# Late tokens of the output and down projections: the high and the low part of the activations in one product of 512 columns

## What is computed

```python
mix = jnp.concatenate([attn, pooled.astype(attn.dtype)], axis=-1) @ p['w_out']
x = x + gt1 * mix
h2 = rms_norm(x, p['norm2_g']) * (1.0 + sc2) + sh2
x = x + gt2 * conv_ffn(h2, p['w_up'], p['conv_w'], p['conv_b'], p['w_down'])
```

## Time and profile before

| | |
|---|---|
| time, median of 3 runs | 1441.02 us (1440.68 to 1443.09) |
| span of the profiled execution | 1439.4 us |
| lowest time of a run less this span | 1.3 us |
| TensorE (PE) busy | 1407.3 us, 98% |
| VectorE (DVE) busy | 903.1 us, 63% |
| ScalarE (ACT) busy | 534.1 us, 37% |
| GpSimd (POOL) busy | 400.5 us, 28% |
| DMA | 147.05 MB, mean 102 GB/s |

### The profile page before, as it was taken

One profiled execution on the slowest core, in us unless ns is written; L12 is line 12 of the kernel. 1 busy time (PEld: TensorE's weight loads), 2 busy tenths in 40 slices (PEclk: granted clock), 3 DMA queues, 4 the chain that ended last, 5 costly groups with the idle time before them and its releaser, 6 DMA issues.

```text
span 1439.4 us, 25053 instructions
## 1 busy us (share of the span) xinstructions
PE 1407.3 (98%) x9905; PEld 1353.2 (94%) x9905; DVE 903.1 (63%) x1429; ACT 534.1 (37%) x798; POOL 400.5 (28%) x273
## 2 busy tenths in 40 slices
PE   6999999999999999999999999999999999999997
PEld 4888889999999999999999977999999999999997
DVE  4448869897966478785775787369744323444333
ACT  5436862533231123232242587344233112232322
POOL 0264002153440033433205800214433101323321
PEclk9999999999999999999999999999999999999999
DMA  9752005253535334335423200224323312222321
GB/s 315 248 178 80 1 2 161 81 166 106 164 121 162 94 117 145 120 120 153 120 58 86 63 1 2 59 89 132 104 79 90 87 57 67 73 73 73 101 61 74
DMA packets 198158, 147.05 MB, mean 102 GB/s; under 512 B 4400, under 2 KB 187448, under 8 KB 197048
## 3 DMA queue, kind: packets, MB, share of 16 engines
q1 hardware_dynamic: 196592, 144.27, 32.8%
q10 hardware_dynamic: 1480, 1.57, 0.3%
HBM read 142.94 MB, written 2.88 MB: 101 GB/s over the span
## 4 chain that ended last, share of the span: by engine, by line
PE 87%; DVE 7%; ACT 2%; issue 2%; SPq 1%; DMA 1%; DVEq 0%; ACTq 0%
PE pair L1468 68%; PE pair L1484 7%; PE pair L1865 3%; PE pair L1910 3%; PE pair L1879 2%; DVE mod_acc L1050 1%; DVE in_lo L1116 1%; DVE norm_t L1106 1%; SPq L414 1%; DVE conv L1390 1%; DMA w_first<-in_w_mod_dram 1%; DVE w_lo L1027 1%; DVE small L1328 1%; PE pair L1768 1%; PE pair L1720 1%
## 5 line engine op out<-in xcount | busy, mean ns | idle before, releaser
L1468 PE MATMUL pair<-in_hi,w_hi 128*128 128x384 f32 x1728 | 396.1, 310 | 0.2
L1468 PE MATMUL pair<-in_lo,w_hi 128*128 128x384 f32 x1728 | 394.7, 309 | 0.0
L1468 PE MATMUL pair<-in_hi,w_lo 128*128 128x384 f32 x1728 | 392.7, 308 | 0.0
L1390 DVE SCALAR_TENSOR_TENSOR conv<-pair,vec,conv 128x127 f32<-128x127 f32 x352 | 168.7, 541 | 193.4 <-ACT conv L935 192.9
L1468 PEld LDWEIGHTS pair<-in_hi,w_hi 128*128 128x128 f32 x1728 | 265.4, 189 | 5.6 <-issue 2.2
L1468 PEld LDWEIGHTS pair<-in_lo,w_hi 128*128 128x128 f32 x1728 | 265.6, 189 | 0.0
L1468 PEld LDWEIGHTS pair<-in_hi,w_lo 128*128 128x128 f32 x1728 | 263.6, 188 | 0.0
L636 POOL TENSOR_TENSOR silu_a<-silu_a,conv 128x640 f32<-128x640 f32 x44 | 113.0, 2567 | 534.2 <-DVE conv L1390 534.2
L935 ACT ACTIVATE conv<-pair,vec 128x640 f32<-128x640 f32 x88 | 77.8, 886 | 407.5 <-PE pair L1468 405.3
L1027 DVE TENSOR_TENSOR w_lo<-w_raw,w_hi 128x1024 fp32r<-128x1024 f32 (+1 forms) x148 | 195.7, 1322 | 38.4 <-ACT w_hi L658 37.9
L658 ACT ACTIVATE w_hi<-w_raw 128x1024 fp32r<-128x1024 f32 (+1 forms) x82 | 96.9, 1182 | 287.1 <-PE pair L1468 270.5
(11 more groups left out here) (205 smaller groups left out, 1775.5 us busy)
## 6 DMA issues: line engine op xcount, KB each, us to landing
w_raw<-in_w_up_dram SPq DMA_DIRECT2D x88, 512.0 KB, 3.8
mod_raw<-in_w_mod_dram SPq DMA_DIRECT2D x64, 512.0 KB, 4.4
w_raw<-in_w_down_dram SPq DMA_DIRECT2D x32, 704.0 KB, 4.6
w_raw<-in_w_in_dram SPq DMA_DIRECT2D x20, 512.0 KB, 4.2
w_first<-in_w_mod_dram SPq DMA_DIRECT2D x16, 512.0 KB, 8.8
w_raw<-in_w_out_dram SPq DMA_DIRECT2D x16, 512.0 KB, 4.1
mod_raw<-in_w_mod_dram SPq DMA_DIRECT2D x4, 1024.0 KB, 5.1
mod_acc<-in_w_mod_dram SPq DMA_DIRECT2D x4, 1024.0 KB, 5.0
```

Of the source, the lines that this page charges most:

```text
L1390: ins = dve.scalar_tensor_tensor(out=conv[:, s, d0:d1], in0=up_result(g, j, s)[:, d0 + sh:d1 + sh], scalar=v(L, V_TAP[t], s * NF + g * FG ...
L1468: ins = pe.matmul(dst[:, a:e], w[:, s, k, :], rhs[:, kk, a:e], start=first and r == 0, stop=last and r == 2)
```

## The change

In the output and down projections, and there only in the tiles that `linear` made (tiles 0 to 5 where a norm follows, 0 to 7 otherwise), the two passes with w_hi over tokens 384 to 639 become one matmul. Its moving operand is the high and the low part of these 256 tokens side by side (for which the two SBUF tensors become one, `in_parts` and `act_parts`), 512 columns, and its result is a whole PSUM bank: columns 0 to 255 of it take w_hi * high (and later w_lo * high), columns 256 to 511 take w_hi * low alone. Five matmuls for one block k, 1,920 columns as before. The low product of the late tokens is thus no longer summed in PSUM with the rest: VectorE adds it to x by an instruction of its own, 256 columns wide, ahead of the two that were there, and the second of these waits for it. `last_two`, `first_three`, the input and up projections and the attention stay.

```diff
+    LATE = T - EDGE
...
-            in_hi = sb("in_hi", [P, NK, T], F32R, at=inputs)
-            in_lo = sb("in_lo", [P, NK, T], F32R, at=inputs)
+            in_parts = sb("in_parts", [P, 2, NK, T], F32R, at=inputs)
+            in_hi, in_lo = in_parts[:, 0, :, :], in_parts[:, 1, :, :]
...
-                act_hi = sb("act_hi", [P, FG, T], F32R, at=own)
-                act_lo = sb("act_lo", [P, FG, T], F32R, at=own)
+                act_parts = sb("act_parts", [P, 2, FG, T], F32R, at=own)
+                act_hi, act_lo = act_parts[:, 0, :, :], act_parts[:, 1, :, :]
...
+        both = [pair[i][:, LIN0 + EDGE:LIN0 + EDGE + 2 * LATE].rearrange("p (r t) -> p r t", r=2) for i in range(2)]
+        late_low = [pair[i][:, LIN0 + T:LIN0 + T + LATE] for i in range(2)]
...
-            def residual(N, s, L, ch, m):
+            def residual(N, s, L, ch, m, g=None):
 
                 dve.wait_ge(s_lin, N + 1)
+                at = n_xlow(L, g, m)
+                dve.scalar_tensor_tensor(out=x[:, m, EDGE:T], in0=late_low[s], scalar=mod[:, L, ch, 1, m:m + 1],
+                                         in1=x[:, m, EDGE:T], op0=ALU.mult, op1=ALU.add).then_inc(s_xlow, 1)
                 for ci, a, b in SEG:
+                    if ci == 1:
+                        dve.wait_ge(s_xlow, at + 1)
                     ins = dve.scalar_tensor_tensor(out=x[:, m, a:b], in0=lin[s][:, a:b],
...
+            def linear_two(n, s, nk, parts, wait_k=None, order=None):
+
+
+                pe.wait_ge(s_wlo, n + 1)
+                order = list(order or range(nk))
+                for k in order:
+                    if wait_k is not None:
+                        wait_k(k)
+                    first, last = k == order[0], k == order[-1]
+                    for r in range(2):
+                        pe.matmul(lin[s][:, 0:EDGE], w_hi[:, s, k, :], parts[:, r, k, 0:EDGE], start=first and r == 0,
+                                  stop=False)
+                    pe.matmul(both[s], w_hi[:, s, k, :], parts[:, :, k, EDGE:T], start=first, stop=False)
+                    for a, e in HALVES:
+                        ins = pe.matmul(lin[s][:, a:e], w_lo[:, s, k, :], parts[:, 0, k, a:e], start=False, stop=last)
+                ins.then_inc(s_lin, 1)
...
-                    linear(tile_out(L) + m, m % 2, NK, in_hi, in_lo, wait_k=out_wait if m == 0 else None,
-                           order=range(NQ) if m == 1 else out_order)
+                    linear_two(tile_out(L) + m, m % 2, NK, in_parts, wait_k=out_wait if m == 0 else None,
+                               order=range(NQ) if m == 1 else out_order)
...
-                        linear(down + m, m % 2, FG, act_hi, act_lo,
-                               wait_k=(lambda k: pe.wait_ge(s_alo, done + k + 1)) if m == 0 else None)
+                        linear_two(down + m, m % 2, FG, act_parts,
+                                   wait_k=(lambda k: pe.wait_ge(s_alo, done + k + 1)) if m == 0 else None)
```

More of the change, by code:

```diff
@@ L228, in build @@
                 conv = sb("conv", [P, 2, T], at=own)
-                act_hi = sb("act_hi", [P, FG, T], F32R, at=own)
-                act_lo = sb("act_lo", [P, FG, T], F32R, at=own)
+                act_parts = sb("act_parts", [P, 2, FG, T], F32R, at=own)
+                act_hi, act_lo = act_parts[:, 0, :, :], act_parts[:, 1, :, :]
                 silu_a = sb("silu_a", [P, T], at=own)
-                w_own_up = [act_lo[:, :, :].rearrange("p g t -> p (g t)")[:, T + i * NK * P:T + (i + 1) * NK * P]
+                w_own_up = [act_lo.rearrange("p g t -> p (g t)")[:, T + i * NK * P:T + (i + 1) * NK * P]
                             .rearrange("p (k n) -> p k n", k=NK) for i in range(6)]
@@ L268, in build @@
         s_lin, s_free = sem("lin_done"), sem("lin_free")
+        s_xlow = sem("x_late_low_added")
         s_gain, s_mfirst = sem("gain_ready"), sem("first_used")
@@ L364, in up_result, with n_xlow @@
             return lin[2 + s if g == 0 and isinstance(j, int) and j == 1 else s]
+        def n_xlow(L, g, m):
+            return L * (3 * NK - 4) + (m if g is None else NK - 2 + g * NK + m)
         def e_of(n):
@@ L945, in up_iter @@
                         act_e.activation(silu_a[:, :], conv[:, 0, :], ACT.Silu).then_inc(s_silu, 1)
-                    up_iter(0, tile_up(L, g) + 2, NK)
-                    up_iter(1, tile_up(L, g) + 4, NK)
+                    for j in range(2):
+                        up_iter(j, tile_up(L, g) + 2 * j + 2, NK)
                     with act_e.Fori(2, FG - 1) as j:
@@ L1416, in _ @@
                     for m in range(NK - 2 if g == NG - 1 else NK):
-                        residual(down + m, m % 2, L, 5, m)
+                        residual(down + m, m % 2, L, 5, m, g)
                         if down + m + 2 < DEPTH * PER_LAYER:
```

## The result

The changed kernel takes 1443.77 us (median of 20 runs, 1442.12 to 1445.26), the kernel before 1441.75 us in the same comparisons (20 runs, 1440.49 to 1443.77). The ratio is 1.0014, with a 95% interval of 1.0007 to 1.0020: slower by 0.14%, some 2.0 us, and less than the 0.2% that the prediction took for the bound. It had said 1439.7 us, 1.3 us faster: the sign is wrong. That 1443.8 still lies inside its range, which ends at 1444.0, is no merit of its sum: the range had been stretched towards the third rival.

What follows compares the result with a forecast made beforehand. PE was taken to bound the kernel, with VectorE setting the pace in layer 0's output projection. PE's -3.5 and VectorE's +2.2 gave -1.3 us, so 1441.0 becomes 1439.7 us; range 1436.8 to 1444.0.

Steps and rivals of the forecast that it cites:

- third rival: Down-tile blocks: wide streams dearer per column, 512 at 233.3 ns, 384 at 176.7; +3.4 us, 1444.4 us; chance 0.11.
- the price of the wide matmul: Edited PE blocks: a matmul of 512 columns was put at 213.3 + 13.3 = 226.7 ns.
- The flat 13.3: PE matmul streams: each matmul costs 13.3 ns beyond its columns at 2.4 GHz, whatever its width.
- The saving on PE: Output and down projections: one matmul of six fewer per block, 10 ns saved in each of 352 blocks, 3.5 us.
- first rival: Edited blocks: the price is mostly gone in the wide product; at 20 ns saved, -4.8 us, 1436.2 us; chance 0.13.
- second rival: Edited blocks: nothing to speak of saved, -2 to 5 ns; +0.4 to +2.9 us, 1442.3 us at 2.5 ns; chance 0.14.
- VectorE in layer 0: Output projection of layer 0: the extra additions lie on the path, +2.2 us, period 8.55 us in place of 8.14.
- The covers: Down projections and layer 1's output projection: extra additions of 0.41 us hidden by ScalarE's wait, VectorE's idle time and slack.
- The two runs of 256 columns: Wide matmul's operand: its two halves lying apart in SBUF cost nothing, read from a near case of 592 ns both ways.
- The clock: Output projection of layer 0: more PE idle time could lower the granted clock; +1.8 us, 1442.8 us and up; chance 0.03.
- Span and time: Whole kernel: the median of the runs was taken as 1.6 us above the span, 1438.1 us becoming 1439.7 us.

Runs made afterwards that it cites:

- experiment 3: Changed kernel with down tiles from the second on replaced by streams of matmuls of one width or other orders, results left out; 1445.5 us, one time.
- experiment 7: Changed kernel plus a GpSimd wait in layer 1, another order of the five matmuls, and layer 0's output projection undone; 1439.44 us against 1441.26, ratio 0.9989.
- experiment 2: Changed kernel with layer 0's output projection back to six matmuls and two additions; 1440.38 us against 1440.76, ratio 0.9999.
- experiment 9: Changed kernel once more, no edit, for a second trace; 1441.52 us beside 1442.13 for the kernel before, one run each.
- experiment 8: Changed kernel with down tiles replaced by streams of more fp32r widths and of bfloat16, results left out; 1446.35 us, one time.
- experiment 5: Changed kernel with one more GpSimd wait, letting VectorE's low weights go first in layer 1; 1441.96 us against 1441.26, ratio 1.0005.

## Why the prediction was wrong

- **The step that failed is the price of the wide matmul:** "The flat 13.3 fits three of four streams, so I take 213.3 + 13.3 = 226.7 for 512 columns." It takes 233.4 (experiment 3). The 384 of the same stream had been at 176.7 in the earlier trace rows, and I charged that to one of three. Of the three streams that "fit", 256 columns alone say nothing about wider ones. The mix in `linear` gives 13.3 by a share of its mean width, 320, just as well, and its 384 was put at 173.4 by subtraction: by the starts in the trace of the kernel before, the matmuls of 384 columns in a down tile take some 176 ns on the average and those of 256 some 117.5. Only `first_three` has 384 columns at 173.3, and no run explains why it is 3.4 ns cheaper there than in `last_two` and in experiment 3. In the changed kernel the wide matmul takes 230 to 233 ns, and the rest of the block 643 to 647 where the prediction had 643.3. Of the 10 ns that a slow block lies above the forecast 870, some 6.5 are the wide matmul; the 3.3 ns of a fast block, 873.3, are the wide matmul alone.
- **The saving on PE,** forecast at 10 ns a block and 3.5 us: measured 0 or 6.7 ns a block, by the stream. That was 0.55 us in the first trace of the change, some 1.8 in the second, and 2.05 at most (experiment 7).
- **The third rival** had the right mechanism, "wide streams are dearer per column", its prices of 233.3 and 176.7 within 0.1 ns, and a total of 1444.4 close to the 1443.8 measured. It did not have the right sum: a block of five costs 880 or 873 and not 883.4. In the slow block the 384 and 256 with w_lo take 293 ns together in place of 296.7; in the fast one the two 384s and the wide one are shorter too, 349 and 230 ns. Its total was near by luck: it had +3.4 us over the kernel before where +2.0 was measured, 1.0 of that from a term that it didn't have, and the kernel before stood 0.7 us higher in this comparison than in the three runs that it started from.
- **The first rival,** 20 ns saved a block because the wide matmul hides its price, is out: beyond its columns at 2.4 GHz a matmul of 512 costs 20.1 ns, and one of 256 to 384 costs 13.3 to 16.7.
- **The second rival,** that little is saved, gives 1442.3 with +1.3. Its sum was nearer than the forecast's, since little was saved indeed. The rule of the Trainium skill that stood beside it is right in that the fixed cost is well under 13.3 ns. No run here shows 2.5 ns: a straight line through the streams of 256 and 512 columns leaves 6.6 ns for a matmul of no columns, and the rate of 0.4583 leaves none. The same page ("TensorE: Matmul & The Clock Gate", section "Back-to-back issue gap") gives about 131 ns for a matmul of 512 columns in a sustained stream with weight loads. The trace disagrees: 233.4 ns.
- **VectorE in layer 0:** +2.2 forecast, +2.18 measured, period 8.55 forecast and 8.55 seen; undoing it alone takes it away (experiment 2). Right in size, place and mechanism.
- **The covers:** the down tiles show no wait for the residual or low weights, ScalarE's wait shrank to nothing and PE has no gap; the output projection of layer 1 hides its additions too. Right.
- **The two runs of 256 columns** cost nothing. Right, 233.4 both ways.
- **The clock** stayed at 1.00 in the output projection of layer 0, where PE has 4 us idle now. Right to leave it out.
- **What no step had:** 1.0 us in layer 1, in a stage that the change doesn't touch, half of what was measured in the end. Together: -3.5 forecast on PE became -0.55 to -1.8, +2.2 stayed, +1.0 came in, so +1.4 to +2.7 where 2.0 was measured.
- **Span and time:** the prediction added 1.6 us to its span, from a profile and a median that belong to different executions. In all runs that have both, the time is 1.9 to 2.1 us above the span (1444.26 and 1442.3, for one). That is 0.3 to 0.5 us of the level and nothing of the difference.
- **Open:** what chooses between 873 and 880 ns. Neither code nor order does (the first trace and experiment 9 are one kernel); that it is how a stream meets the engine's state at its start is argued, not shown, though a group that changes its speed behind the transposes speaks for it. Whether neighbours that share an operand change a price, as the 173.3 of `first_three` may say, was not tested by itself. Open too is why one VectorE instruction in layer 1 starts 0.37 us earlier in every kernel with the change. One thing goes with it in the traces: in both of the kernel before, a packet of an instruction queue (q14, 8 KB) starts 0.66 us behind that instruction (777.99 and 777.52), and in the two of the changed kernel that queue has none within 25 us of it. That an instruction fetch moved is a candidate, not shown.

## What to carry to other kernels

Before you merge matmuls to save "per-instruction" cost, time two widths in streams of their own, the new one among them, and look for the row that doesn't fit: with one mean width, a price per instruction and one per column look the same. Take the price of each width from its own starts and not by subtraction from a mix. Here columns cost some 10% more than the clock says, and merging two matmuls saved 6.7 ns at best. An addition to an engine that sets the pace costs what it takes in the queue, 0.4 us here for a record of 0.47, as long as the rows say that the engine has no idle time; so apply such a change only where the engine has slack (experiments 2 and 7). And where two engines alternate closely, compare the order of their instructions in stages that the change doesn't touch: a shift of a few tenths can turn it over.

## What the runs showed of the hardware

- A stream of fp32r matmuls with a weight load each took 0.456 to 0.469 ns a column from 256 to 512 columns at a granted clock of 1.00 (experiments 3 and 8), and some 111.5 ns at 128, 192 and 224 columns alike. In `first_three`, where the products follow each other in another order, 384 columns took 0.451 ns a column. bfloat16, read from the same words at a stride of two for both operands, took 6 to 7 ns less at 256, 384 and 512 columns.
- VectorE's subtraction of two SBUF operands, 1.23 us by itself, took 2.49 us when GpSimd's addition of two SBUF operands had started 0.18 us ahead of it, and 1.23 again as soon as GpSimd was made to wait (experiment 5). The other way round, GpSimd's addition took 2.48 us in place of 1.58 when VectorE had started 0.19 us ahead. The Trainium skill says so ("SBUF — State Buffer", section "Who interferes with whom"): a VectorE instruction with two SBUF inputs contends with a GpSimd one that reads SBUF, the port pair that they share is an exclusive lock, and the order of issue decides which of them is blocked. The trace agrees: 1.26 us more for VectorE, near the 1.40 that were left of GpSimd's step, and 0.90 more for GpSimd, near the 1.04 that were left of VectorE's.
- The same code had down tiles of 9.61 us in one trace where it had 9.68 in another: 0.07 us a tile, 1.2 us in all between the two traces of the changed kernel, and steady over a group as long as nothing lies between its tiles.
